# Decoder step on one core: three layer norms, and the projections that follow them, in another order

## The reference

```python
def layer_norm(x, g, b):
    mu = jnp.mean(xf, axis=-1, keepdims=True)
    var = jnp.mean(jnp.square(xf - mu), axis=-1, keepdims=True)
    return ((xf - mu) * lax.rsqrt(var + LN_EPS)).astype(x.dtype) * g + b

def sq_relu_mlp(x, w1, w2):
    return jnp.square(jax.nn.relu(x @ w1)) @ w2
...
        h = layer_norm(DN_ALPHA * h + mix, ln_g[i, 0], ln_b[i, 0])
        h = layer_norm(DN_ALPHA * h + sq_relu_mlp(h, mlp_w1[i], mlp_w2[i]), ln_g[i, 1], ln_b[i, 1])
```

## Time and profile before

| what | value |
|---|---|
| runs | 2039.76, 2048.35 and 2225.68 us, median 2048.35 us |
| profiled execution | 2044.02 us, span 2042.3 us |
| PE busy | 1910.1 us, 94% of the span |
| DVE, ACT, POOL busy | 836.1, 704.0 and 906.4 us |
| mean granted TensorE clock | 0.959 of full speed |

### The profile page before, as it was taken

The page is one execution under the profiler, slowest core; times in us unless marked ns, Lnnn a source line. Parts: engine busy times, 40 slices in busy tenths (PEclk is TensorE's granted clock), DMA queues, the critical chain, the costliest instruction groups (busy, mean ns, idle before and its releaser), DMA issues. The chain is left out here.

```text
span 2042.3 us, 36493 instructions
## 1 busy us (share of the span) xinstructions
PE 1910.1 (94%) x14678; PEld 1741.1 (85%) x14678; DVE 836.1 (41%) x1605; ACT 704.0 (34%) x1292; POOL 906.4 (44%) x652
## 2 busy tenths in 40 slices
PE   8999989889889989999999989799879899999996
PEld 7987878768789989999979989555459799999996
DVE  6375867765662200121331121587455421012134
ACT  5473636533232211222231130466443422122222
POOL 3444344333476633564543333454205565346552
PEclk9999989989989999999989989799999899999997
DMA  5213113131322263322212433600431122222221
GB/s 188 73 52 125 52 56 121 52 150 52 111 73 72 82 175 85 125 82 83 83 42 82 152 107 102 227 1 1 146 125 62 52 82 83 82 83 82 82 76 64
DMA packets 61221, 185.13 MB, mean 91 GB/s; under 512 B 15662, under 2 KB 20430, under 8 KB 59568
## 3 DMA queue, kind: packets, MB, share of 16 engines
q1 hardware_dynamic: 50432, 130.92, 19.7%
q0 software_dynamic: 9952, 50.08, 6.9%
q10 hardware_dynamic: 720, 2.49, 0.3%
HBM read 167.05 MB, written 27.35 MB: 95 GB/s over the span
## 5 line engine op out<-in xcount | busy, mean ns | idle before, releaser
L1310 PE MATMUL dense<-xs,split 128*128 128x288 f32 x6784 | 962.7, 300 | 14.3 <-POOL xs L816 7.9
L1310 PEld LDWEIGHTS dense<-xs,split 128*128 128x128 f32 x6784 | 928.2, 191 | 47.0 <-issue 33.9
L704 POOL TENSOR_TENSOR split<-ring,split 128x1024 fp32r<-128x1024 f32 x174 | 443.4, 2549 | 617.2 <-ACT split L952 617.2
L952 ACT ACTIVATE split<-ring 128x1024 fp32r<-128x1024 f32 x212 | 224.0, 1056 | 786.9 <-PE dense L1310 765.5
L1310 PE MATMUL dense<-hid,split 128*128 128x288 f32 x3072 | 414.1, 297 | 5.9 <-POOL split L704 5.9
L1310 PEld LDWEIGHTS dense<-hid,split 128*128 128x128 f32 x3072 | 412.5, 190 | 6.1 <-POOL split L704 6.1
L1899 DVE SCALAR_TENSOR_TENSOR tile<-tile,dense 128x576 f32<-128x576 f32 (+1 forms) x56 | 42.2, 754 | 412.5 <-PE dense L1310 407.1
L2088 DVE TENSOR_SCALAR sq<-dense 128x576 f32<-128x576 f32 x64 | 48.5, 758 | 308.5 <-PE dense L1310 306.1
L925 POOL TENSOR_SCALAR tile<-tile,tile,tile 128x128 f32<-128x128 f32 (+3 forms) x128 | 77.7, 623 | 82.2 <-DVE tile L2251 82.2
L744 POOL TENSOR_TENSOR tile<-tile,tile 128x512 f32<-128x512 f32 (+1 forms) x20 | 25.9, 1294 | 197.9 <-DVE tile L1961 197.8
L1887 DVE SCALAR_TENSOR_TENSOR tile<-tile,tile,tile 128x512 f32<-128x512 f32 x72 | 76.2, 1058 | 23.9 <-ACT tile L1033 22.2
(11 more groups left out here) (322 smaller groups left out, 2089.6 us busy)
## 6 DMA issues: line engine op xcount, KB each, us to landing
ring<-in_w SPq DMA_DIRECT2D x212, 512.0 KB, 3.3
tile<-in_state POOLq DMA_DIRECT2D x4, 2048.0 KB, 8.8
o_sssm<-tile POOLq DMA_DIRECT2D x4, 2048.0 KB, 7.9
tile<-in_cmp POOLq DMA_DIRECT2D x32, 256.0 KB, 3.2
tile<-in_win POOLq DMA_DIRECT2D x8, 1024.0 KB, 6.0
tile<-in_sel SPq DMA_DIRECT2D x32, 256.0 KB, 5.3
o_kv<-tile POOLq DMA_DIRECT2D x1, 3456.0 KB, 13.7
bskew<-bscr SPq DMA_DIRECT2D x1, 3072.0 KB, 22.5
```

What stands on the lines that cost most here:

```text
L704: pool.tensor_tensor(split[:, j, 1, :], ring[:, j, :], split[:, j, 0, :].bitcast(F32), ALU.subtract).then_inc(w_split, 1)
L952: act.activation(split[:, j, 0, :], ring[:, j, :], ACT.Copy).then_inc(w_hi, 1)
L1310: mm = pe.matmul(dense[:, 2 * par + h_, 0:HT], split[:, j, w, cols], v[:, kk, h_ * HT:(h_ + 1) * HT], start=kk == 0 and t == 0, stop=kk == ...
```

## The change

For norms 0, 1 and 2 the next projection no longer reads the normalized stream. While the projection ahead of the norm still runs, ACT rounds xT times the norm's scale g (raw_hi) and DVE takes the rest (raw_lo); two columns, g and b themselves, stand behind the 576 tokens, so a block's second half has 290 columns and its last two hold W·g and W·b. raw_projection multiplies this raw stream: the first block's high products, then the sums by token, then its low products; the second block's high products, then the spread of the factor, then its low products. As each block leaves its banks, raw_block on DVE copies the two columns (gb), forms mean x W·g minus the block, and multiplies by the factor; the shift and the sign follow (in a relu on ACT in M1, in a tensor_scalar on DVE for K/V and q). The normalized xT is still wanted as residual and for the second half of M1: normalize does one chunk for every two blocks on DVE, and ACT (normalized) and POOL (x_los) do scale, shift and split at the start of M2, where ACT and POOL also split the weight slots. position_sums, the gates' operand and position_columns go behind the q projection. bias_tables goes behind the first two blocks of M2, and SP's wait for it (s_bias) moves by 4 slots. POOL's copies of bias rows and its K/V splits change places. Norm 3 has the same operations as before.

```diff
+        xs_wide = split_tile("xs", xs_at, 2, KC, T + 2)
+        xs = xs_wide[:, :, :, 0:T]
+        xs_end = xs_at + 2 * KC * (T + 2)
...
+                def raw_hi(m):
+                    if m == 0:
+                        if k == 2:
+                            act.wait_ge(outs, 64)
+                        act.activation(RAW[k][:, 0, :, T], lng[:, k, :], ACT.Copy)
+                        act.activation(RAW[k][:, 0, :, T + 1], lnb[:, k, :], ACT.Copy)
+                    if m == KC - 1:
+                        act.wait_ge(blk_evac, b0 + KC)
+                    act.activation(RAW[k][:, 0, m, 0:T], xT[:, m, :], ACT.Copy, scale=lng[:, k, m:m + 1]
+                                   ).then_inc(xh_ready, 1)
...
-                    if 1 <= m < KC - 1:
+                        if k < 3:
+                            raw_hi(0)
+                    if m == KC - 1 and k < 3:
+                        raw_hi(m)
+                    if m:
                         square(m)
+                        if k < 3 and m < KC - 1:
+                            raw_hi(m)
...
+            def normalized(k, m, x=None):
+                act.wait_ge(ln_scaled, 2 * (k * KC + m + 1))
+                ends = dict(bias=lnb[:, k, m:m + 1], scale=lng[:, k, m:m + 1])
+                if x is not None:
+                    act.activation(x[:, 0, m, :], xT[:, m, :], ACT.Identity, **ends).then_inc(xh_ready, 1)
+                act.activation(xT[:, m, :], xT[:, m, :], ACT.Identity, **ends).then_inc(x_ready, 1)
...
+                        if half == 0:
+                            act.wait_ge(raw_step, i * 3 * NSLOT + (3 * (N_RAW[2 * k] + j) + 2))
+                            act.activation(sq[:, j, :], sq[:, j, :], ACT.Relu, bias=gb[:, 1:2], scale=-1.0
+                                           ).then_inc(raw_step, 1)
...
+                    s0 = S_M2[k][0] + 2
+                    act.wait_ge(w_used, S_M2[k][0])
+                    for m in range(5):
+                        normalized(2 * k, m, XM[k])
+                    split_hi(s0)
+                    for m in range(5, KC):
+                        normalized(2 * k, m, XM[k])
+                    split_hi(s0 + 1)
+                    split_his(s0 + 2, end)
...
             split_his(S_KV + 2, S_O + 2)
+            for m in range(KC):
+                normalized(1, m)
...
+                                n = HT + 2 * raw * h_
+                                mm = pe.matmul(dense[:, 2 * par + h_, 0:n], split[:, j, w, cols],
+                                               v[:, kk, h_ * HT:h_ * HT + n],
                                                start=kk == 0 and t == 0, stop=kk == nsl * KC - 1 and t == 2)
...
+            def raw_projection(k, b0, s0, blocks):
+                hi, lo = RAW[k][:, 0], RAW[k][:, 1]
+                for j in range(2):
+                    pe.wait_ge(blk_evac, b0 + j - 1)
+                    pe.wait_ge(w_split, s0 + j + 1)
+                    for later in range(2):
+                        for kk in range(KC):
+                            if j == 0 and later:
+                                pe.wait_ge(x_split, RAW_LO[k] + kk + 1)
+                            elif j == 0:
+                                pe.wait_ge(xh_ready, RAW_HI[k] + kk + 1)
+                            for t, (w, v) in enumerate(((0, lo),) if later else ((0, hi), (1, hi))):
+                                for h_ in range(2):
+                                    n = HT + 2 * h_
+                                    mm = pe.matmul(dense[:, 2 * ((b0 + j) % 2) + h_, 0:n],
+                                                   split[:, (s0 + j) % NSLOT, w, kk * P:(kk + 1) * P],
+                                                   v[:, kk, h_ * HT:h_ * HT + n],
+                                                   start=kk == 0 and t == 0 and not later,
+                                                   stop=kk == KC - 1 and later == 1)
+                        if not later:
+                            (token_sums, spread_scale)[j](k)
+                    mm.then_inc(w_used, 1)
+                with pe.Fori(1, blocks // 2) as i:
+                    for j in range(2):
+                        dense_block(b0 + j, s0 + j, 1, hi, lo, i, 2, raw=1)
...
                 for cols in (slice(0, 512), slice(512, T)):
-                    mm = pe.matmul(flat_s[:, cols], ones[0:TQ, :], SQS[k][0:TQ, cols], start=True, stop=True)
+                    mm = pe.matmul(flat_s[:, cols], ones[0:TQ, :], CEN[k][0:TQ, cols], start=True, stop=True)
                 mm.then_inc(ln_wide, 1)
...
+                raw_projection(2 * k, B_M1[k][0], S_M1[k][0], H1)
+                projection(B_M2[k][0], S_M2[k][0], KC, 2, *HID[k], (hid_ready, 2 * k * H1),
+                           between=bias_tables if k == 0 else None)
+                pe.wait_ge(x_split, NORM_LO[k] + KC)
+                projection(B_M1[k][1], S_M1[k][1], H1, 1, XM[k][:, 0], XM[k][:, 1])
+                last_projection(2 * k + 1, *HID[k], (hid_ready, (2 * k + 1) * H1))
...
+            raw_projection(1, B_KV, S_KV, SL_KV)
+            projection(B_Q, S_Q, SL_Q, 1, xs_wide[:, 0], xs_wide[:, 1], raw=1)
+            pe.wait_ge(blk_evac, B_O - 1)
+            pe.wait_ge(s_cw1, 16)
+            position_sums(0, 32)
...
+            position_columns()
...
+                for j in range(2):
+                    dve.wait_ge(x_split, NORM_LO[k] + j + 1)
+                    residual(b0 + j, j, ALPHA, s0 + (j + 1) * 2)
...
+                    if k in (1, 2):
+                        for q in range(0 if m == 2 else m - 1, m):
+                            raw_lo(k, q)
+                if k < 3:
+                    for m in range(KC) if k == 0 else (KC - 1,):
+                        raw_lo(k, m)
+            def raw_lo(k, m):
+                dve.wait_ge(xh_ready, RAW_HI[k] + m + 1)
+                if m == 0:
+                    for q, v in enumerate((lng, lnb)):
+                        dve.tensor_tensor(RAW[k][:, 1, :, T + q], v[:, k, :], RAW[k][:, 0, :, T + q].bitcast(F32),
+                                          ALU.subtract)
+                dve.scalar_tensor_tensor(RAW[k][:, 1, m, 0:T], xT[:, m, :], lng[:, k, m:m + 1],
+                                         RAW[k][:, 0, m, 0:T].bitcast(F32), ALU.mult, ALU.subtract
+                                         ).then_inc(x_split, 1)
...
-                dve.tensor_tensor(SQS[k][0:TQ, :].rearrange("p (c j) -> p c j", c=TC),
+                dve.tensor_tensor(CEN[k][0:TQ, :].rearrange("p (c j) -> p c j", c=TC),
...
+            def normalize(k, m, i=None):
+                xm = xT[:, at_step(m, i, 1), :]
+                dve.tensor_tensor(xm, xm, row[:, :], ALU.subtract).then_inc(ln_scaled, 1)
+                dve.wait_ge(ln_scaled, at_step(2 * (k * KC + m) + 1, i, 2))
+                dve.tensor_tensor(xm, xm, flat_s, ALU.mult).then_inc(ln_scaled, 1)
...
+            def raw_block(k, n, b0, s0, j, i=None, keep=False):
+                first = i is None and n == N_RAW[k] and j == 0
+                if first:
+                    dve.wait_ge(ln_wide, 2 * k + 1)
+                    link(dve, "dve", dve.tensor_copy(row[:, :], flat_x))
+                h = sq[:, j, :]
+                dve.wait_ge(w_used, at_step(s0 + j + 1, i, 2))
+                dve.tensor_copy(gb[:, :], dense[:, 2 * j + 1, HT:HT + 2]).then_inc(raw_step, 1)
+                dve.wait_ge(raw_step, at_step(3 * (n + j) + 1, i, 6))
+                dve.scalar_tensor_tensor(halves(h), halves(row[:, :]), gb[:, 0:1], dense_out(j), ALU.mult, ALU.subtract
+                                         ).then_inc(raw_step if keep else blk_evac, 1)
+                if keep:
+                    dve.wait_ge(raw_step, at_step(3 * (n + j) + 2, i, 6))
+                else:
+                    dve.wait_ge(blk_evac, at_step(b0 + j + 1, i, 2))
+                if first:
+                    dve.wait_ge(ln_wide, 2 * k + 2)
+                dve.tensor_tensor(h, h, flat_s, ALU.mult).then_inc(raw_step, 1)
...
-                dve.wait_ge(blk_evac, at_step(B_M1[k][half] + j + 1, i, 2))
+                if half:
+                    dve.tensor_scalar(halves(h), dense_out(j), 0.0, None, ALU.max).then_inc(blk_evac, 1)
+                    dve.wait_ge(blk_evac, at_step(B_M1[k][half] + j + 1, i, 2))
+                else:
+                    n = N_RAW[2 * k]
+                    raw_block(2 * k, n, B_M1[k][0], S_M1[k][0], j, i)
+                    dve.wait_ge(raw_step, at_step(3 * (n + j) + 3, i, 6))
...
+                if half == 0:
+                    normalize(2 * k, 0)
...
+                        normalize(2 * k, 0, i)
...
+            def kv_block(j, i=None):
+                h = raw_block(1, N_RAW[1], B_KV, S_KV, j, i, keep=True)
+                dve.tensor_scalar(kvT[:, at_step(j, i, 2), :], h, gb[:, 1:2], -1.0, ALU.subtract, ALU.mult
+                                  ).then_inc(blk_evac, 1)
+                dve.wait_ge(blk_evac, at_step(B_KV + j + 1, i, 2))
...
```

(17 more changed lines are left out.)

246 lines of the change are left out of this document (116 added, 130 removed).

## The result

The changed kernel takes 2020.51 us (median of 4 runs, 2017.36 to 2028.92) against a median of 2048.39 us for the kernel before. The ratio, which leaves out the one disturbed run of before (2225.68 us), is 0.9892, 95% interval 0.9857 to 0.9927. That is 22 us less, 15 to 29 by the interval: clear of noise, but under the 2% that the prediction took as the bar for "faster". The quotient of the two medians alone would be 0.9864; the longer series of later runs, in which the kernel before has medians of 2041 to 2043 us, agree with the ratio. The forecast was 2017. The profiled execution spans 2015.7 us, 26.6 less than before; the forecast of its sum was 26.8 less. It is the fastest of the four runs of after, so its 26.6 is a little more than the runs gained.

A forecast was written before the change was run, and what follows sets the result against it. PE, busy 94%, was taken to bound the kernel, with 61.4 us to win at three norms. Less 14.1 that stays, the gain was 47.3; costs of 20.5 left 26.8, so 2044.0 became 2017 us, range 1998 to 2038.

The forecast's parts named there:

- What stays on PE: Three norms: sums by token, spreads of mean and factor, and a wait of 1.0 still cost PE 14.1 us.
- the wait for raw_lo: Norm 0: PE's low products wait for the last raw_lo on DVE, about 0.9 us, taken as 1.0.
- The wait at M2: Start of M2's first half: PE waits 3.5 us for ACT's chunks and POOL's split, once per layer, 7.0 in all.
- The clock behind it: After each wait at M2's start the lower clock loses 2.5 us, twice, 5.0 in all.
- bias_tables and the late slot: bias_tables behind one residual more costs 0.8 us; the late slot moves with SP's wait, priced at nothing.
- Behind q: After the q projection: eight normalized chunks and a copy lengthen ACT's chain, costing 6.5 us.
- ACT's chain sets the end there: Behind q: ACT's chain sets the end, and the position sums, some 7 us on PE, lie beside it.
- The two columns: 52 raw blocks: two more columns per matmul cost 1.2 us in all.
- A: Rival: the clock falls in each norm too, 2.5 us more lost per norm, 2024 us; chance 0.16.
- B: Rival: no wait at M2, as POOL's and ACT's work overlaps better, 12.0 us less, 2005 us; chance 0.17.
- C: Rival: the raw read-out on DVE paces PE, a pair taking up to 15.4 us, 2085 us; chance 0.07.
- D: Rival: no gain in one norm, its statistics later than the second block's high products, 2031 us; chance 0.05.

The follow-up runs named there:

- m2_spread: Changed kernel with the normalized chunks ahead of M2's first slots spread 2, 3 and 3 before three slots, not 5 and 3 before two: 2012.0 us.
- place: Changed kernel with gb behind the arena, streams and hidden tiles starting 112 bytes into a block of 128, stream chunks 592 columns apart: 2009.01 us.
- late_sums: Changed kernel with the sums by token and the mean's spread behind the first raw block's low products, not between high and low: 2033.74 us.
- q_spread: Changed kernel with norm 1's eight normalized chunks on ACT spread over the eight q blocks instead of behind the last: 2019.08 us.
- map: Changed kernel plus 3072 matmuls behind its end, reading moving rows at 32 starts with other engines idle: 131.6 to 136.2 ns per matmul.
- before_place: Kernel before with its streams and hidden tiles 24 bytes further on (112 into a block of 128 bytes), nothing else: 2031.66 us.
- best: Changed kernel with the edits of place, m2_spread and q_spread together: 1995.27 us, 0.9764 of the kernel before.
- gb_moved: Changed kernel with gb allocated behind the arena instead of ahead of it, pitch of 578 columns kept: 2017.46 us.
- cols296: As place, with the second half of the raw products 296 columns wide instead of 290: 2003.89 us.

## Why the prediction was right, step by step

- **What stays on PE: right.** Forecast 14.1 us over the three norms; measured 52.66 less six blocks of 6.40 is 14.3. Norm 0 had the wait for raw_lo: 0.86 us by the starts of the matmuls where 0.9 was worked out and 1.0 taken, and norm 0 is 0.9 longer than norms 1 and 2. The sums take 0.96 and 1.02 from start to start, as the 0.97 was read. The statistics did hide: the diagonal was ready at 604.0, the spread of the factor was issued at 606.9.
- **The wait at M2: right.** 3.34 and 3.43 us where 3.5 was forecast, by the chain named; m2_spread removed it. The next slot was in time, as said; by the sum's own terms POOL has it split at 22.4 (16.3 + 3 x 1.2 + 2.55) and not at 22.1, and it was 22.5.
- **The clock behind it: mechanism right, size less.** Half for 3.4 us each, 1.7 lost, not 2.5. A third stretch of the same length came at 737, inside M2 behind bias_tables, and was not forecast.
- **bias_tables and the late slot.** bias_tables holds PE for 5.19 us in both kernels, so the 0.8 for it came to nothing but for that stretch of clock. The late slot moved to 782.9 and costs 5.58 us instead of 5.90: priced at nothing, rightly.
- **Behind q: near in size, by luck in part.** Forecast 6.5; measured 6.2 to the compression and 4.6 behind it. The step "ACT's chain sets the end there" failed, if by little. It was true of before, where PE stood idle 4.96 us in the transposes; the 7.2 us of position sums that the change puts there take up that idle time, and then PE comes last, 0.64 us behind ACT. The sentence that called them "beside" ACT's chain should have added PE's work up on its own: 7.2 + 9.6 is as long as ACT's 6.1 + 10.5. On top came 3.0 us of half clock in the gates, which no term foresaw; without them ACT would have been the later one. The sign that was named, DVE's wait some 6 us longer, came out as 16.11 against 12.34, 3.8 longer.
- **The two columns: mis-sized, and not the only thing.** 1.2 us was priced by columns counted. In fact 290 columns keep a raw block at 6.44 in place where 296 give 6.36, and gb's two floats and the pitch of 578 moved the starts of all moving rows: some 32 M1 blocks x 0.04, 16 M2 blocks x 0.2 and 16 x 0.12, 52 raw blocks x 0.04, together about 8.5 us (an estimate from these block times) instead of 1.2. Nothing in the diff's arithmetic shows this; the allocation line does.
- **What made up for it: luck.** Attention came out 5.2 us shorter and the mixer 2.4 longer, in stretches that the change hardly touches. The time at half clock differs there from trace to trace (in attention 30.7 us in m2_spread, 34.1 in after, 40.9 in before), which makes 3.4 of the 5.2 and 1.7 of the 2.4; what makes the rest is not shown. The sum hit 26.6 against 26.8 partly because +7 and -5 met, and by the ratio of the runs, 22 us with 15 to 29 as its interval, the forecast may be some 5 us too good.
- **The rivals.** A did not happen in the profiled execution of after: the clock was 1.00 in all three norms. But it is close, and it does not hang on a wait. In late_sums half clock followed six waits of 1.5 us together. In m2_spread and q_spread, whose norm 1 is that of the changed kernel, the clock fell for 3.4 us right behind the sums by token and the spread of the mean, though PE had gone on without a gap (in m2_spread from 1034.47), and norm 1 took 18.73 us instead of 17.22. B did not happen, though the edit for it is small. C did not: DVE waited 0.98 and 2.38 us for PE in each pair of raw blocks, so the read-out had over 3 us of room, as taken. D did not.

The window behind the sums by token of norm 1 in m2_spread, where PE is busy throughout and the clock is 0.57:

```profile
1042.00:1046.00 4.00, 4.00 (x21) 4.00 (x20) 1.60 (x4) 0.23 (x1) 0.00 (x0) 0.57 0.00 0
```

## What to carry to other kernels

A norm between two projections need not be a seam: if the next projection is linear, multiply the raw stream and correct the product, and let the reductions stand between the passes of the first blocks, where something independent covers the slowest operand. When a step is moved to a place where an engine waits, add up the work of each engine there afterwards, the waiting one too; of two chains of nearly one length either can set the end. And when a change adds a tile or widens a row, compare the time of a steady block before and after on work that it did not touch: an allocation can cost as much as an instruction.

## What the runs showed of the hardware that was not expected

- A matmul of 128 rows by 288 float32 columns, one after another with new weights each, takes 131.6 to 136.2 ns at the full clock by where its moving rows start in SBUF (map); 112 bytes into a block of 128 were best (131.6), then 48 and 64 (132.1 and 132.2). In this kernel that is worth 10 to 12 us to the old version (before_place) and 11 to 14 to the new one (place).
- The start is not all: M2 in place ran at 12.64 us a block in one layer and at 12.80 behind the wait in the other, from starts of 240 in both, and at 216 the map's blocks took 134.0 ns on average where the kernel before has 133.4. The rate can change within one tile: in place the second layer's matmuls on hid stand at 131.6 ns up to the wait at 1687 and at 133.3 behind it, and in best, where that wait is gone, they keep 131.7; in gb_moved they go from 134.5 to 133.3 at 1707, where PE does not wait. What decides was not tried.
- A second half of 296 columns is faster than one of 290 (6.36 against 6.44 us a block, cols296 and place).
- Six waits of 0.2 to 0.5 us, spread over 4 us, were followed by half clock (late_sums, 0.74 and then 0.50); two waits of 0.2 were not (place, norm 0).
- The granted clock also fell with PE busy and no gap before it: at 1177.4 in after, behind 64 matmuls of one output row and into 80 of 48 columns, and at 1042.1 in m2_spread, behind 24 sums of one column each and the spread of the mean.
